# Where a per-head softmax merge is fetched, multiplied and split in a hybrid decoder layer

## The reference

```python
def dilated_attention(q, k, v):
    outs, lses = [], []
    for g, (window, dilation) in enumerate(DILATED_GROUPS):      # (128,1), (512,4), (2048,16)
        o, lse = dilated_group(q[:, :, g], k, v, window, dilation)
        outs.append(o)
        lses.append(lse)
    w = jax.nn.softmax(jnp.stack(lses, axis=0), axis=0)
    o = jnp.sum(w[..., None] * jnp.stack(outs, axis=0), axis=0)
    return o.astype(v.dtype)
```

## Time and profile before

| what | value |
|---|---|
| runs | 1859.98, 1861.59, 1866.5 us (median 1861.59) |
| profiled execution | 1866.5 us, its span 1864.9 us |
| granted TensorE clock | 0.992 of full speed |
| busy share of the span | PE 96%, PEld 82%, DVE 58%, ACT 38%, POOL 26% |
| phase A, heads | `stat_sb` is copied at 203.8 us in the first head, at 576.1 us in the last: 124.1 us a head |
| phase B, first head | from about 576 us |
| DMA | 196.33 MB, 105 GB/s over the span |

### The profile page before, as it was taken

How to read it: one execution, slowest core, us unless ns; L and a number is a source line. 1 busy time by engine, 2 the same in 40 slices (tenths; PEclk the granted TensorE clock), 3 DMA queues, 4 the chain that set the end, 5 groups by cost and what they waited for, 6 DMA issues and landing times. The chain is left out here.

```text
span 1864.9 us, 27248 instructions
## 1 busy us (share of the span) xinstructions
PE 1795.3 (96%) x9188; PEld 1521.7 (82%) x9188; DVE 1082.6 (58%) x1928; ACT 703.3 (38%) x1598; POOL 486.8 (26%) x578
## 2 busy tenths in 40 slices
PE   6999998999999999999998999999999999999999
PEld 6888887988887888888876888878888888878887
DVE  4362452643734849485765554596555555566776
ACT  5334242333333335353535213353333233334443
POOL 2010001101114424150602000006565556520120
PEclk9999999999999999999999999999999999999999
DMA  7311321423222111111117224322323223278764
GB/s 204 90 43 55 92 86 46 119 67 89 76 73 76 51 35 38 42 45 45 39 55 255 87 73 123 124 74 91 112 84 118 101 96 107 85 262 306 255 214 175
DMA packets 169292, 196.33 MB, mean 105 GB/s; under 512 B 9553, under 2 KB 119473, under 8 KB 168705
## 3 DMA queue, kind: packets, MB, share of 16 engines
q1 hardware_dynamic: 156816, 163.13, 27.4%
q0 software_dynamic: 6128, 21.74, 3.5%
q10 hardware_dynamic: 6272, 10.49, 1.5%
HBM read 150.88 MB, written 44.45 MB: 105 GB/s over the span
## 5 line engine op out<-in xcount | busy, mean ns | idle before, releaser
L2237 PE MATMUL bank<-act_hi,w_hi 128*128 128x512 f32 x568 | 230.6, 406 | 4.0 <-DVE act_lo L1871 3.7
L2239 PE MATMUL bank<-act_hi,w_lo 128*128 128x512 f32 x568 | 223.6, 394 | 0.0
L2238 PE MATMUL bank<-act_lo,w_hi 128*128 128x512 f32 x568 | 223.4, 393 | 0.0
L2237 PE MATMUL bank<-ca,wq 128*128 128x512 f32 x528 | 207.2, 392 | 5.4 <-DVE wq L1982 3.0
L2239 PE MATMUL bank<-ca,wq 128*128 128x512 f32 x528 | 206.5, 391 | 0.0
L2238 PE MATMUL bank<-ca,wq 128*128 128x512 f32 x528 | 206.4, 391 | 0.0
L2237 PE MATMUL bank<-w_hi,act_hi 128*128 128x256 f32 (+1 forms) x576 | 180.6, 314 | 2.1 <-DVE act_lo L1554 2.1
L2239 PE MATMUL bank<-w_hi,act_lo 128*128 128x256 f32 (+1 forms) x576 | 177.4, 308 | 0.0
L2238 PE MATMUL bank<-w_lo,act_hi 128*128 128x256 f32 (+1 forms) x576 | 177.4, 308 | 0.0
L1538 DVE TENSOR_TENSOR w_lo<-w_raw,w_hi 128x1024 fp32r<-128x1024 f32 x38 | 46.1, 1224 | 157.2 <-ACT w_hi L1002 157.2
L2237 PEld LDWEIGHTS bank<-act_hi,w_hi 128*128 128x128 f32 x568 | 108.0, 190 | 27.8 <-DVE act_lo L1871 4.8
(11 more groups left out here) (357 smaller groups left out, 4226.7 us busy)
## 6 DMA issues: line engine op xcount, KB each, us to landing
w_raw<-in_w_in SPq DMA_DIRECT2D x60, 512.0 KB, 4.2
rawd<-in_w_ffn_down SPq DMA_DIRECT2D x99, 256.0 KB, 5.2
rx<-y_scratch SPq DMA_DIRECT2D x77, 256.0 KB, 4.4
wr<-in_w_ffn_gate SPq DMA_DIRECT2D x11, 1024.0 KB, 5.4
wr<-in_w_ffn_up SPq DMA_DIRECT2D x11, 1024.0 KB, 5.4
y_scratch<-sq SPq DMA_DIRECT2D x11, 1024.0 KB, 4.3
y_scratch<-yq SPq DMA_DIRECT2D x33, 256.0 KB, 2.0
gate_scratch<-gbuf ACTq DMA_DIRECT2D x32, 256.0 KB, 2.1
```

The lines of the kernel that those rows point to most:

```text
L2237: pe.matmul(ps, lhs_hi, rhs_hi, start=first, stop=False, skip_group_check=onto)
L2238: pe.matmul(ps, lhs_hi, rhs_lo, start=False, stop=False, skip_group_check=onto)
L2239: return pe.matmul(ps, lhs_lo, rhs_hi, start=False, stop=last, skip_group_check=onto)
```

## The change

Four things are changed, all within the merge and the tables of phase A, and in the first head of phase B.

1. The four kinds of merge DMA leave SP for ACT: the statistics are stored right behind the copy to `stat_sb`, loaded at stage 0 of the next head; the weights are stored at stage 4 and loaded at stage 5. In phase B: stages 0, 2 and 3. SP's head loop becomes a hardware loop with weight tiles and v alone.
2. `merge_mul` 0 and 1 move from stages 8 and 9 to stages 6 and 7, inside `qk_norm`, between the weight subtraction and the norm; number 2 moves from 12 to 8. The copies to `u_t` wait for all three.
3. `HI_A`: the casts and subtractions of tiles 5 to 9 move from stages 8, 10, 11, 13, 14 to 7, 8, 10, 11, 12.
4. `EXP_AT` goes: ACT takes the exponentials of a unit directly behind the copy of that step. Unit 0 is exponentiated at stage 6 instead of 7, unit 1 at 7 instead of 8.

```diff
-    HI_A = {6: [4], 8: [5], 10: [6], 11: [7], 13: [8], 14: [9]}
-    EXP_AT = {7: [0], 8: [1, 2]} | {s: UNITS_AT[s] for s in range(9, 16)}
+    HI_A = {6: [4], 7: [5], 8: [6], 10: [7], 11: [8], 12: [9]}
...
-        for h in range(1, H):
+        with sp.Fori(1, H) as h:
             for k in range(4):
                 load_a(h, k)
             sp.wait_ge(pv_ready, NB * h)
-            alone(sp)
-            store_stats(sp, h - 1)
-            load_stats(sp, h - 1)
             load_vt(h)
             for k in range(4, 8):
                 load_a(h, k)
-            store_weights(sp, h - 1)
-            load_weights(sp, h - 1)
...
                         act.copy(o, i_).then_inc(pt_evac, 1)
-                for j in EXP_AT.get(s, []):
                     if j < NB:
                         act.wait_ge(neg_max, NB * h + j + 1)
...
+                if behind and s == 0:
+                    load_stats(act, h - 1)
                 if behind and s == 1:
                     act_weights(h - 1)
+                if behind and s == 4:
+                    store_weights(act, h - 1)
+                if behind and s == 5:
+                    load_weights(act, h - 1)
...
             act.copy(stat_sb[:, :], pt_ps[0:2 * NU, 0:P]).then_inc(stat_sbd, 1)
+            store_stats(act, h)
...
+                if not tail and s == 0:
+                    load_stats(act, H - 1)
                 if not tail and s == 1:
                     act_weights(H - 1)
+                if not tail and s == 2:
+                    store_weights(act, H - 1)
+                if not tail and s == 3:
+                    load_weights(act, H - 1)
...
                 if behind and j == 3:
                     merge_norm(h - 1)
+                if behind and j in (6, 7):
+                    merge_mul(h - 1, j - 6)
                 dve.wait_ge(t1_rstd, n + 1)
...
-                    if behind:
-                        dve.wait_ge(wb_mul, 3 * h - 2 + b // 4)
+                    dve.wait_ge(wb_mul, 3 * h)
...
-            MUL_AT = {8: 0, 9: 1, 12: 2}
...
-                    if behind and s in MUL_AT:
-                        merge_mul(h - 1, MUL_AT[s])
+                    if behind and s == 8:
+                        merge_mul(h - 1, 2)
```

More of the change, by code:

```diff
@@ L367, in load_stats @@
         eng.wait_ge(stat_out, 16 * h + 16)
-        alone(eng)
         eng.wait_ge(c_wgt, 3 * h)
@@ L567, in _ @@
                 load_a(h, k)
-            store_weights(sp, h - 1)
-            load_weights(sp, h - 1)
-        def load_b(h, k):
+        with sp.Fori(0, H) as h:
             cols = [C_KB + P * h, C_QB + P * h, C_VB + DV * h + P, C_VB + DV * h,
                     C_RB + DV * h, C_RB + DV * h + P]
[L574 to L585, removed]
             for k in range(TB):
-                load_b(h, k)
+                free(B0 + TB * h + k)
+                load(B0 + TB * h + k, k, w_in[:, :, bass.ds(cols[k], P)])
         def load_m(n):
```

## The result

| what | before | after |
|---|---|---|
| median of the runs | 1863.54 us (1859.98 to 1866.5, 4 runs) | 1882.4 us (1879.29 to 1884.12, 4 runs) |
| profiled execution, span | 1866.5, 1864.9 us | 1880.51, 1878.8 us |
| `stat_sb` copied, first and last head | 203.8, 576.1 us | 200.3, 589.6 us |
| from there to the end of the span | 1288.8 us | 1289.2 us |

The change makes the kernel slower: after over before is 1.0104, 95% interval 1.0084 to 1.0125, that is +19.4 us (15.7 to 23.3) where +3.8 was forecast (1865.4 us, range 1858 to 1872). The median of before has moved up since the prediction, with a fourth run of 1865.49 us. The profiled pair differs by 13.9 us (spans), and the table's last two rows say where: up to the end of the first head 3.5 us are gained, heads 1 to 3 (counted from 0, so the second to the fourth) lose 17.0, and everything behind the attention heads together loses 0.4.

A forecast was written before the change was run, and what follows sets the result against it. PE, busy 96% of the span, was taken as the bound, so only its waits counted. Terms of -7.8, +6.6 and +5.0 us made +3.8 on the median of 1861.6, giving 1865.4 us, range 1858 to 1872.

The forecast's parts named there:

- What bounds the kernel: PE, busy 96% of the span; edits on ACT, DVE or SP count only by changing a wait of PE.
- Term 1: Phase A, four heads: casts leave stages 13 and 14, saving 3.45 us less a new 1.5 at stage 12; -7.8 us.
- Term 2: Stages 6 to 9, three heads: DVE and ACT take turns, PE waits 2.2 us behind stream 9; +6.6 us.
- Term 3: First head of phase B, once: DVE waits 4.9 us for `wb`, all of it reaching PE; +5.0 us.
- nothing catches up: First head of phase B: DVE runs without a gap afterwards, so PE keeps the whole 4.9 us delay.
- The -0.2 us inside the term: First head of phase B: the multiply takes 1.22 us without POOL instead of 1.43 beside it; -0.2 us.
- What the DMAs add in phase A I cost at nothing: Phase A: statistics loads, `wb` load and a store 0.6 us ahead of two casts fit in slack; 0 us.
- PE waiting at stage 1 for a subtraction: Sign that the forecast is wrong, at stage 1: the store on ACT costs more than its slack.
- Slower: Rival: turn-taking in stages 6 to 9 costs 4.0 us a head; +9.2 us, 1870.8 us; 0.33 with larger phase B delays.
- The faster rival: Casts hidden at stage 12 (-13.8 us), turn-taking in stages 6 to 9 nearly so; -5.8 us, 1855.8 us; chance 0.10.

The follow-up runs named there:

- e9: Kernel before with the new `HI_A` and the multiplies at stages 6, 7 and 8, exponentials as before, all DMAs on SP: 1852.31 us, ratio 0.9928.
- e8: Kernel before with the new `HI_A` alone, multiplies and exponentials in their old places: 1867.51 us, ratio 1.0014.
- e5: Kernel before, all DMAs on SP, with 64 semaphore increments added to the body of ACT's head loop: 1869.46 us, ratio 1.0021.
- e7: Kernel before with only the merge DMAs in the first head of phase B moved to ACT, at stages 0, 2 and 3: 1866.92 us, ratio 1.0021.
- e1: Kernel before with the three tables changed (casts, multiplies, exponentials) and all merge DMAs left on SP: 1863.82 us, ratio 0.9986.
- e4: Changed kernel with ACT's head loop written out instead of branching back, DMAs where the change put them: 1863.31 us, ratio 0.9985.
- e12: Changed kernel with ACT's head loop written out and `EXP_AT` as in before, every DMA where the change put it: 1851.46 us, ratio 0.9923.
- e6: Changed kernel with the eight statistics loads given back to SP, whose head loop is written out: 1867.74 us, ratio 1.0017.
- e3: Changed kernel with SP's load of v held back as long as in before: 1874.46 us, ratio 1.0042.
- e11: Kernel before with only `HI_A` changed: tiles 5 and 6 at stage 8, 7 and 8 at stage 9, 9 at stage 11: 1843.88 us, ratio 0.9889.

## Why the prediction was wrong

**What bounds the kernel.** Right. Every difference is a wait of PE on ACT or DVE, or PE's clock after one.

**Term 1, -7.8 us.** Right in place and size as far as waits go. In e9, where it stands alone, PE's waits for `u_t` and `pt` are 11.0 us against 19.0, so -8.0; the new wait at stage 12 is 1.32 us (1.5 forecast), the rest at stage 14 1.07 (1.0 forecast). In the changed kernel it is -6.6: the third and fourth head have a further wait for `u_t` of 0.9 us each, which I did not follow to its cause. It is right only together with the multiplies' move: the new `HI_A` alone (e8) adds 2.8 us of waits. The forecast priced the whole change, and had not seen that this term hangs on the other. The ratio of e9 says -13.4 us (-10.1 to -16.6), more than the waits that went. The difference is the clock. Before, stretches of 5 us in which PE ran below full speed:

```profile
195.00:200.00 5.00, 5.00 (x18) 3.98 (x19) 0.42 (x1) 0.00 (x0) 0.00 (x0) 0.66 0.00 0
...
315.00:320.00 5.00, 2.07 (x13) 1.54 (x12) 1.56 (x2) 2.27 (x4) 0.00 (x0) 0.90 0.14 52
320.00:325.00 5.00, 5.00 (x20) 4.16 (x20) 0.42 (x1) 0.00 (x0) 0.00 (x0) 0.76 0.02 3
...
565.00:570.00 5.00, 3.39 (x13) 2.65 (x14) 1.99 (x3) 0.95 (x3) 0.00 (x0) 0.82 0.09 32
570.00:575.00 5.00, 5.00 (x22) 4.11 (x21) 0.00 (x0) 0.16 (x1) 0.00 (x0) 0.84 0.00 0
```

Each time PE had just waited behind stream 14, and each time it lost 1.7 us (5 x 0.34; 5 x 0.10 + 5 x 0.24; 5 x 0.18 + 5 x 0.16), together 5.1. In e9 no stretch between 80 and 600 us is below 1.00. Waits and clock give -8.0 - 5.1 = -13.1 us, and the ratio says -13.4. That they meet so closely is in part luck, since the clock's share is not fixed: e5 and e7, with the tables of before, lose 3.4 us to such stretches in phase A, in other heads. I had priced a wait at its own length only.

**Term 2, +6.6 us.** Right: 6.5 us in three waits up to 2.2 us, behind stream 9 of heads 1 to 3, none in head 0. Its cost on the clock was missing here too: in e1 stretches below full speed follow it in the third and fourth head, 1.7 us each, and two more follow the wait of 1.32 us behind stream 12. Together 6.9 us, more than the 5.1 of before, so e1's clock takes back what its waits gain.

**Term 3, +5.0 us.** The delay is right: DVE waits 3.87 to 3.95 us for `wb`, and PE's wait for the mask is 4.6 us longer in e7 and 3.6 in the changed kernel, whose PE shows

```profile
632.09 3.33 PE L2423 MATMUL lvl_ps<-fbuf 128*128 128x128 f32 x14 [4.93 <-DVE lvm L1789]
```

The size for the sum is off by the sentence that nothing catches up: PE's next wait for a mask, 2.4 us in before, is used up. By waits the term is +2.1 us in e7. In the changed kernel the profiled pair shows +0.4 us for all that follows phase A, but that stretch scatters by some us. Over all traces, from the last copy to `stat_sb` to the end of the span, it is 1287.5 us on average in the seven kernels where SP issues these DMAs in phase B (1285.8 to 1290.7) and 1290.0 in the seven where ACT does (1289.2 to 1291.0): +2.6 us, half of the forecast. The -0.2 us inside the term came: the first multiply takes 1.22 us in e7, with POOL's last piece of work done at 613.21, where it took 1.43.

**The step that failed: "What the DMAs add in phase A I cost at nothing".** I priced the store on ACT at 0.6 us ahead of two casts, and the casts as just in time. That is what e4 and e12 show, where ACT's loop is written out: 0.55 us of idle time, no wait for `w_lo`. In the changed kernel the first cast stood 7.05 and 7.36 us. The 23 rows that the DMAs add to a pass of ACT's loop are why, and not the transfers by themselves: e5 shows it with instructions that touch no data, e6 by taking 17 away. The early load of v, which I had not followed either (SP was freed of the merge, so it issues it 8 us earlier), more than doubles the price: less the 1.2 us that e6 has without a fetch, 2.7 us in e3 and 5.9 here. The cost is 11.9 us of waits and 4.1 us of clock. I named the symptom ("PE waiting at stage 1 for a subtraction"), with the wrong cause beside it.

The Trainium skill, Runtime: NRT & Kernel Launch, Instruction fetch mechanics, says that code is brought in by DMA block after block, and that a taken branch whose target has left the window forces a fetch before the engine goes on. The traces agree, with idle stretches of 2.5 to 7.4 us at the return. By its figures, blocks of 256 instructions held two at a time, a body of 195 should fit. Instructions that only set registers come on top of my count: with them the traces have 261 records of ACT a pass in before, 273 in e6, 299 in the changed kernel and 325 in e5. All are under 512, so the size of the window alone does not say which body is fetched anew, and no run here shows what does. It was the rule that spoke against this change, and I had not weighed it.

**Rivals and chances.** Slower was right, at 0.33, but by neither mechanism given for it. The faster rival's mechanism is not borne out either. It had the wait at stage 12 gone, for -13.8 us; e9 comes to -13.4 with that wait in place (1.32 us), by the clock that nobody had priced. Only e11, which keeps casts out of stage 12, has no such wait.

**What stays open.** Of the 17.0 us that heads 1 to 3 lose in the profiled pair, 16.0 come at the loop's returns; the tables' terms add 1.9 in waits and the clock gives 1.7 back (one stretch of half clock elsewhere against two), so 0.8 us have no row. The time of e7 leaves term 3 between 1.1 and 6.7 us. Of the 3.85 us in e3 against 2.51 in e5, most is the store, which stands in the one stretch and not in the other: less what each place takes without a fetch (1.19 us in e6, 0.29 in before) it is 2.7 against 2.2.

## What to carry to other kernels

When a change adds instructions to the body of a hardware loop, count them as a cost of their own and look in the trace for the packets of the code queue at the loop's return: an idle stretch ended by "issue" right there, absent at the first entry and with such packets beside it, was code being fetched in this kernel, and writing the loop out (e4) or moving a few instructions to another engine (e6) removed it. Price a wait of PE at its length, and set the half clock that can follow it (0 or 1.7 us behind the short waits here) as a bound beside it. And where edits share a stage (a cast, a multiply, POOL's additions set off by it), lay out their combinations, since each alone can have the other sign.

## What the hardware showed that I had not expected

- The fetch at a loop's return: 2.5 us of idle time in e5, 3.85 in e3, 7.05 and 7.36 beside the load of v, of which 0.3 us in e5, and by e6 1.2 us in the others, stand there without a fetch too. Four packets (0.03 MB) in 20 us of trace are its only other mark.
- DVE's instruction on 128x2 numbers takes 0.17 us, and 1.99 us beside POOL's additions on 128x1024 (e8). The Trainium skill, GPSIMD Engine Reference, Specifications, tells of interfaces to SBUF shared by the two, for Vector instructions in a two-port mode or with two SBUF inputs. This one has one tile as its input; it stood until POOL's addition was done, to 0.02 us. No run here shows whether it ran in a two-port mode.
- The half clock behind a wait costs 1.7 us each time in before, 1.8 and 2.3 behind the 6 us waits of the changed kernel. It does not follow every wait: e9 keeps waits of 1.3 and 1.1 us in its heads and never leaves 1.00, e4 leaves it once and e1 twice behind one of 1.3, and before left it in three of four heads.
